# A mixer's hand-written order: low-rank gates a tile sooner, keys times decay as an event of its own, chunk products a part later, the states' last two reads a tile sooner with buffers of their own

## The reference

```python
h = modulate(rms_norm(x, g_norm1[l]), shift1, scale1)
proj = h @ w_in[l]
sb_q, sb_k, sb_v, gq, gk, gv, gg, gf = jnp.split(proj, offsets, axis=-1)
o_sb = stick_breaking_attention(...)                       # 8 heads of 64
log_alpha = jax.nn.log_sigmoid(gf @ w_fg2[l] + b_fg2[l]) / GLA_TAU
o_gla = gla_chunk_causal(gq, gk, gv, log_alpha)            # 4 heads, 8 chunks of 64 tokens
oh = oh * lax.rsqrt(jnp.mean(oh * oh, axis=-1, keepdims=True) + EPS)
o_gla = (oh * g_gla_out[l]) * jax.nn.silu(gg)
mixed = jnp.concatenate([o_sb, o_gla], axis=-1) @ w_out[l]

# inside gla_chunk_causal
k_dec = kc * jnp.exp(total[:, :, None] - cum)              # keys times decay
chunk_kv = jnp.einsum('bnchk,bnchv->nbhkv', k_dec, vc)     # chunk products
state = decay[..., None] * state + kv
o = jnp.einsum('bnchk,nbhkv->bnchv', qc, states)           # the states' reads
```

## Time and profile before

| what | us |
| --- | --- |
| median of 3 runs | 1533.07 (1532.12 to 1535.98) |
| the profiled execution, its own time | 1533.55 |
| span of its instructions | 1531.8 |
| PE busy | 1480.5 (97%) |
| DVE, ACT busy | 785.8 (51%), 550.9 (36%) |
| granted TensorE clock, mean | 0.977 of 2.4 GHz |
| the mixer's events, first tile to the first matmul of the output projection | 852.9 to 1099.4 |

### The profile page before, as it was taken

How to read it: one execution, slowest core, us unless ns; L and a number is a source line. 1 busy time by engine, 2 the same in 40 slices (tenths; PEclk the granted TensorE clock), 3 DMA queues, 4 the chain that set the end, 5 groups by cost and what they waited for, 6 DMA issues and landing times.

```text
span 1531.8 us, 18223 instructions
## 1 busy us (share of the span) xinstructions
PE 1480.5 (97%) x6646; PEld 1199.9 (78%) x6646; DVE 785.8 (51%) x1013; ACT 550.9 (36%) x699; POOL 25.0 (2%) x48
## 2 busy tenths in 40 slices
PE   6999999999999999999999896999899999999998
PEld 5887888888888888888888774666677888888886
DVE  7345454466455454544555654454356653563564
ACT  4343212223234413323143423335334542552342
POOL 1000000000000000000000000000000000000000
PEclk8999999999999999999999998999899999999998
DMA  5323544334432344352422221111022232323221
GB/s 172 109 88 107 176 160 156 123 116 163 161 110 86 107 129 146 104 170 82 150 83 83 83 79 31 55 56 55 28 83 82 85 107 82 110 93 98 90 76 55
DMA packets 135789, 158.18 MB, mean 103 GB/s; under 512 B 2513, under 2 KB 129071, under 8 KB 135743
## 3 DMA queue, kind: packets, MB, share of 16 engines
q1 hardware_dynamic: 129024, 131.08, 26.4%
q0 software_dynamic: 6240, 26.30, 5.1%
q10 hardware_dynamic: 479, 0.17, 0.0%
HBM read 155.44 MB, written 2.10 MB: 103 GB/s over the span
## 4 chain that ended last, share of the span: by engine, by line
PE 93%; DVE 3%; ACT 2%; DMA 1%; issue 1%; SPq 0%; DVEq 0%; ACTq 0%
PE bank L436 29%; PE bank L438 28%; PE bank L437 28%; DMA raw<-in_w_in 1%; ACT weights_hi L784 1%; PE bank L716 1%; PE aux L471 1%; PE aux L716 1%; PE aux L740 1%; PE aux L458 1%; PE aux L505 1%; PE aux L651 0%; DVE weights_lo L1113 0%; PE aux L546 0%; PE bank L726 0%
## 5 line engine op out<-in xcount | busy, mean ns | idle before, releaser
L436 PE MATMUL bank<-operand_hi,weights_hi 128*128 128x512 f32 x1936 | 767.3, 396 | 8.1 <-DVE operand_lo L1125 5.5
L438 PE MATMUL bank<-operand_hi,weights_lo 128*128 128x512 f32 x1936 | 758.2, 392 | 0.0
L437 PE MATMUL bank<-operand_lo,weights_hi 128*128 128x512 f32 x1936 | 758.0, 392 | 0.0
L436 PEld LDWEIGHTS bank<-operand_hi,weights_hi 128*128 128x128 f32 x1936 | 366.6, 189 | 93.2 <-issue 16.8
L438 PEld LDWEIGHTS bank<-operand_hi,weights_lo 128*128 128x128 f32 x1936 | 366.1, 189 | 77.6
L437 PEld LDWEIGHTS bank<-operand_lo,weights_hi 128*128 128x128 f32 x1936 | 366.9, 189 | 75.2 <-issue 1.0
L1113 DVE TENSOR_TENSOR weights_lo<-raw,weights_hi 128x1024 fp32r<-128x1024 f32 (+1 forms) x244 | 296.1, 1214 | 172.9 <-ACT weights_hi L784 167.3
L784 ACT ACTIVATE weights_hi<-raw 128x1024 fp32r<-128x1024 f32 (+1 forms) x244 | 253.6, 1045 | 300.5 <-PE bank L438 300.1
L789 ACT ACTIVATE operand_hi<-value 128x512 f32 (+1 forms) x90 | 56.9, 633 | 128.8 <-DVE value L1301 34.0
L1123 DVE TENSOR_TENSOR operand_lo<-value,operand_hi 128x512 fp32r<-128x512 f32 (+1 forms) x90 | 62.0, 689 | 42.5 <-ACT operand_hi L789 42.5
L1543 DVE SCALAR_TENSOR_TENSOR conv_or_gate<-bank,vector_table,conv_or_gate 128x511 f32<-128x511 f32 x44 | 32.9, 747 | 80.9 <-ACT conv_or_gate L1070 79.0
(11 more groups left out here) (206 smaller groups left out, 697.6 us busy)
## 6 DMA issues: line engine op xcount, KB each, us to landing
raw<-in_w_in SPq DMA_DIRECT2D x40, 1024.0 KB, 5.2
raw<-in_w_ff SPq DMA_DIRECT2D x32, 1024.0 KB, 5.2
ada_or_attention<-in_w_ada POOLq DMA_DIRECT2D x16, 1536.0 KB, 7.7
raw<-in_w_up SPq DMA_DIRECT2D x22, 1024.0 KB, 5.1
raw<-in_w_out SPq DMA_DIRECT2D x8, 1024.0 KB, 5.0
raw<-in_w_down SPq DMA_DIRECT2D x8, 1024.0 KB, 5.0
raw<-in_w_proj_a SPq DMA_DIRECT2D x4, 1024.0 KB, 6.4
raw<-in_w_proj_b SPq DMA_DIRECT2D x4, 1024.0 KB, 6.5
```

What stands on the lines that cost most here:

```text
L436: pe.matmul(dst[:, :], wh, ah, start=(kt == 0), stop=False)
L437: pe.matmul(dst[:, :], wh, al, start=False, stop=False)
L438: mm = pe.matmul(dst[:, :], wl, ah, start=False, stop=(kt == k_tiles - 1))
```

## The change

Five things, all in the mixer:

- `fg 0`, `fg 1`, `fg 2` stand ahead of tiles 5, 6 and 7 where they stood behind them. The two memsets that the scan needs go from tile 5's share of DVE to tile 4's.
- Keys times decay is an event of its own, `k_dec n`, one part ahead of `turn_k n`. For PE and ACT it is empty.
- `kv 0` to `kv 3` come one part later (`kv 0` and `kv 2` at the first part of tiles 15 and 16, `kv 1` and `kv 3` at the third).
- `o 2` and `o 3` go from the second and third part of tile 22 to the first and second part of tile 21, `ms 2` and `ms 3` from tile 23 to (21, 2) and (22, 0), `gated 0` and `gated 1` from (22, 0) to (22, 1).
- `o 2` and `o 3` get buffers of their own, `gk[0]` and `gk[1]` in the space of `mix_bias`, in place of `tA[0]` and `tA[1]`; and since ACT's squares go through `tb(n % 2)`, ACT now waits for L1477 of `ms n - 2` ahead of the square of `o n`.

The number and shapes of the instructions stay. The core of the diff:

```diff
-    others = {(9, 3): [("turn_k", 0)], (10, 3): [("turn_k", 1)],
+    others = {(9, 2): [("k_dec", 0)], (9, 3): [("turn_k", 0)], (10, 2): [("k_dec", 1)], (10, 3): [("turn_k", 1)],
...
-    order += [("tile", 4), ("turn_v", 3), ("tile", 5), ("fg", 0), ("tile", 6), ("fg", 1), ("tile", 7), ("fg", 2)]
+    order += [("tile", 4), ("turn_v", 3), ("fg", 0), ("tile", 5), ("fg", 1), ("tile", 6), ("fg", 2), ("tile", 7)]
...
+        scaled = [tA[0][:, :], tA[1][:, :], gk[0], gk[1]]
...
                 elif kind == "o":
                     act.wait_ge(aux2_filled, AUX2[event] + 1)
+                    if n >= 2:
+                        act.wait_ge(g_scaled, n - 1)
                     act.activation(tb(n % 2), aux[2][:, :], ACT.Square).then_inc(o_sq, 1)
...
-                    if n == 5:
+                    if n == 4:
 
                         dve.memset(spread[:, :], 1.0).then_inc(reset_ready, 1)
...
-                elif kind == "turn_k":
+                elif kind == "k_dec":
                     dve.wait_ge(g_dec, 2 * n + 2)
                     dve.wait_ge(*mix_slot(("gk", n)))
                     dve.tensor_tensor(gate_y[n], gk[n], gate_y[n], ALU.mult).then_inc(k_dec, 1)
+                elif kind == "turn_k":
                     keep_turned(event, k_tok.rearrange("p (b n) -> p b n", b=NBLK)[:, :, n * P:(n + 1) * P])
...
-                    dve.tensor_scalar(tA[n % 2][:, :], aux[2][:, :], col(C_GGLA + n), None, ALU.mult).then_inc(aux2_read, 1)
+                    dve.tensor_scalar(scaled[n], aux[2][:, :], col(C_GGLA + n), None, ALU.mult).then_inc(aux2_read, 1)
```

More of the change, by code:

```diff
@@ L91, in mixer_schedule @@
               (19, 3): 9, (20, 3): 10, (21, 3): 11, (22, 3): 12, (23, 3): 13}
-    others = {(9, 3): [("turn_k", 0)], (10, 3): [("turn_k", 1)],
+    others = {(9, 2): [("k_dec", 0)], (9, 3): [("turn_k", 0)], (10, 2): [("k_dec", 1)], (10, 3): [("turn_k", 1)],
               (11, 1): [("turn_gv", 0)], (12, 1): [("turn_gv", 1)], (13, 1): [("turn_gv", 2)], (14, 1): [("turn_gv", 3)],
[1 row of a table removed]
[1 row of a table added]
               (19, 1): [("o", 0)], (20, 0): [("o", 1)], (20, 1): [("ms", 0)], (20, 2): [("ms", 1)],
[2 rows of a table removed]
[1 row of a table added]
+              (22, 1): [("gated", 0), ("gated", 1)]}
     order = [("tile", 0)]
@@ L1040, in _ @@
                     act.wait_ge(value, VALUED["gla"] + n + 1)
-                    round_operand(0, 4 + n, tA[n % 2][:, :])
+                    round_operand(0, 4 + n, scaled[n])
                 elif kind == "z":
@@ L1473, in _ @@
                     dve.wait_ge(o_sq, n + 1)
-                    dve.tensor_scalar(tA[n % 2][:, :], aux[2][:, :], col(C_GGLA + n), None, ALU.mult).then_inc(aux2_read, 1)
+                    dve.tensor_scalar(scaled[n], aux[2][:, :], col(C_GGLA + n), None, ALU.mult).then_inc(aux2_read, 1)
                 elif kind == "ms":
                     dve.wait_ge(g_inv, n + 1)
-                    dve.tensor_tensor(tA[n % 2][:, :], tA[n % 2][:, :], tb(n % 2), ALU.mult).then_inc(g_scaled, 1)
+                    dve.tensor_tensor(scaled[n], scaled[n], tb(n % 2), ALU.mult).then_inc(g_scaled, 1)
                 elif kind == "gated":
@@ L1482, in _ @@
                         dve.wait_ge(tri_done, N_ITEMS)
-                    dve.tensor_tensor(tA[n % 2][:, :], tA[n % 2][:, :], yb[:, n * S:(n + 1) * S], ALU.mult).then_inc(value, 1)
-                    rest(0, 4 + n, tA[n % 2][:, :], MADE["gla"] + n)
+                    dve.tensor_tensor(scaled[n], scaled[n], yb[:, n * S:(n + 1) * S], ALU.mult).then_inc(value, 1)
+                    rest(0, 4 + n, scaled[n], MADE["gla"] + n)
                 elif kind == "z":
```

## The result

The changed kernel takes 1522.76 us (median of 4 runs, 1521.82 to 1523.59) against 1532.9 us before (4 runs). The ratio is 0.9936 with a 95% interval of 0.9923 to 0.9949: 10 us faster, 8 to 12. The forecast was 9.3 us.

The account below looks back on a forecast made before the run. PE works all but 3% of the span, so gains come only from its gaps and clock. Terms +7.1 - 8.7 - 1.2 - 6.5 = -9.3 gave 1523.8 us from the median 1533.07, range 1517.5 to 1530.

Parts of the forecast that it names:

- three signs of being wrong: No wait before the low-rank product, clock low for longer than 10 us, or a low clock from the `o 3` wait.
- The gates a tile sooner: New 5.4 us gap before the low-rank product: `tri 0` 4.8 us late plus 2.3 of low clock, +7.1.
- Keys times decay: At `turn_k`, waits of 3.5 and 3.6 us and 1.7 of clock go, 0.1 comes back: -8.7 us.
- Chunk products: PE reaches the chunk products a part later, which covers their 1.2 us wait: -1.2 us.
- The last two reads: At `o 3`, a 3.7 us wait and 4.5 of clock go, a new 1.7 us wait comes: -6.5 us.
- Gaps of 1.2 left no low clock: New 1.7 us wait before `o 3` was given no clock cost, with 4.5 us as the other bound.
- The third rival: ACT's chain behind Silu takes 2.8 us more, so `tri 11` waits 1.5: 1525.3 us; chance 0.02.
- The gates come sooner after all: Copy of last v does not hold PE; gate chain starts 5.4 us sooner, +7.1 becomes -0.8: 1516 us; chance 0.05.
- Gains are given back to the clock: Gaps of 5.4, 4.3 and 1.7 us each leave low clock costing 4.5: 1532 us, no change; chance 0.09.
- Slower: Low clock after the low-rank gap does not end, up to `z 1`: about +29 for 2.3, 1550 us; chance 0.04.

Follow-up runs that it names:

- e1: Kernel before with only the gates a tile sooner and their memsets at tile 4: 1537.86 us, ratio 1.0044.
- e5: Changed kernel with DVE's copy of the last turned v ahead of tile 4's share: 1514.83 us, ratio 0.9891 to the kernel before.
- e2: Kernel before with only keys times decay as its own event, one part ahead of `turn_k`: 1523.6 us, ratio 0.9947.
- e6: Kernel before with only the chunk products a part later: 1532.45 us in one run.
- e3: Kernel before with only the last two reads a tile sooner, with their own buffers: 1527.53 us, ratio 0.9966.
- e10: Changed kernel run a third time, unedited: 1525.43 us in one run, against 1530.68 for the kernel before on that chip.
- e7: Changed kernel with gates 0 and 1 in old order and the second gate behind item 1 and `turn_k 0`: 1509.7 us, ratio 0.9851 to before.
- e4: Changed kernel with the gates back in their old order, all else kept: 1515.62 us, ratio 0.9896 to the kernel before.
- e12: Kernel before with only the last two reads sooner, run again unedited: 1525.54 us once, against 1530.24 for the kernel before on that chip.
- e11: Changed kernel with gates in old order, run again unedited: 1517.46 us once, against 1530.24 for the kernel before on that chip.

## Why the prediction was right, point by point

**The whole.** Forecast 1523.8, measured 1522.76. Part of the agreement is luck. In the two profiled executions the mixer gained 8.1 us (212.1 to 204.0), 1.2 less than forecast; the spans differ by 11.8, and the other 3.7 lie outside the mixer, 0.9 ahead of `turn_v 3` and 2.8 behind `pv 11`, where the change moves nothing. The 0.9 is idle time of PE. Behind `pv 11` PE has 3.8 us less busy time at the same matmuls (422.2 to 418.4), with a granted clock of 0.97 before and 0.99 after, and 1.0 more idle time.

Of the three signs of being wrong that the prediction names, two stayed away: the wait before the low-rank product is there, and no low clock in the mixer lasted longer than 10 us (the longest, behind the gap before `o 3`, took 6.8). The third came: the wait before `o 3` did cost a low clock. The time was right all the same, since the miss was small.

**The gates a tile sooner, +7.1 forecast.** The gap was 5.0 where 5.4 was reckoned. The small memset ran beside the copy, and the copy started 1.99 us after the scalings where it was 1.31 before, so 0.7 later and not 0.8; and the transposes end 0.6 us after their start, by their row, where the prediction took 0.4. The clock behind it cost 1.4, not 2.3. `tri 0` came 44.7 us after `turn_v 3` where it was 38.9, 5.7 later (4.8 + 2.3 was forecast), and its wait fell to 4.1, where the prediction had 4.3 (its own terms, 5.1 + 4.8 - 5.4, give 4.5). The clock behind `tri 0`, left at 3.1, was 2.3. The sign, the place and the releaser were right, and e1 alone (6.7 us slower) and e5 (the gap closed by the place of one copy) show the cause.

**Keys times decay, -8.7 forecast.** e2 alone gave 8.1 by the ratio and 10.7 in its mixer, which differs from the forecast also by 1.4 us of clock behind the gap before `o 3` and 0.8 behind `tri 0` that this profile did not have. Both waits went, 0.2 came back where 0.1 was forecast. In the changed kernel the way from `tri 0` to `pv 8` is 10.6 us shorter (132.97 to 122.41); without the 1.2 of the chunk products and the 0.8 of clock behind `tri 0`, 8.6 are left for this part.

**Chunk products, -1.2.** Gone in the changed kernel and in e6.

**The last two reads, -6.5 forecast.** From `pv 8` to `pv 11` it was 40.2 us (1057.82 to 1098.01) and is 37.0: 3.2 gained. This is the term that was mis-sized, in the step "Gaps of 1.2 left no low clock, and this one is nearer to it than to 3.5; I add nothing for it, 4.5 as the other bound". The wait was 1.6 as forecast (1.7), but a low clock followed that cost 3.4 us, within the bound. Over nine profiles it costs 1.3 on the mean, which alone makes the term 5.2. The 4.5 that was to go away was mis-sized too: it is the largest of four profiles with the old gap, whose mean is 3.7. With both means the term is about 4.5. e3 measured 5.2 (3.4 to 7.2), which tells none of these figures from another. `tri 11` did not wait, by 1.4 us where 1.3 was reckoned. The third rival, a longer chain behind Silu, is out: from PE's start of `z 11` to the end of item 11 it took 9.3 us (1068.77 to 1078.05), as in the rows of before, and behind each of the two table loads of 1.28 us the next activation began 1.29 us after the load's start, as before.

**The rivals.** "The gates come sooner after all" fell with the 5.0 us wait, and e5 shows what it would have taken: one copy moved, and then 1514.83, where the rival gives 1516. "Gains are given back to the clock" came true at one of its three gaps, with 3.4 us for its 4.5; at the other two the clock cost 1.4 and 2.3. "Slower" did not: the low clock behind the low-rank gap cost 1.4 us, so it ended within three us of matmuls with 16 columns of weights, and the longest of four profiles was 5.4 us (e10). That rival's price does not come out of its own terms either: 11.1 and as much again, less 4.3, is 17.9 and not 29, and 23 us of low clock would take PE through the product and one tile (22.2 us) and not through three and a half. No run bears on that price.

**What I did not see.** The forecast priced the gates at +7.1 and so said that the change was better without them. Nor did it ask whether `tri 0`'s wait could be had at all, which e7 did: by taking the second gate out from ahead of item 0 and not by moving both.

## What to carry to other kernels

When an in-order engine waits through one shared buffer, moving a step ahead gains nothing if the read that frees the buffer stays where it is in the other engine's queue: look up which instructions stand ahead of that read, and move the read (5.0 us to 0.8 by one copy). Even that only took back the loss here: e5 is no faster than the old order of the gates (e4). The gain lay in what item 0 itself stood behind (e7, 5.1 us to 0.9). A product that one engine needs soon should stand ahead of the housekeeping that needs the latest tile (7.1 us of waits for two reordered instructions). And price the parts of a change one by one: this one was 10 us faster as a whole, with one part that cost 6.

## What the runs showed of the hardware

The four waits of PE in the changed kernel's mixer repeat to 0.1 us over three profiles (5.0, 4.1, 1.6, 0.2); the one at the norm ahead of it does not (2.5, 2.5, 3.0). Nor does the clock: after gaps of 4.1 us and more it was low in all 16 places seen, at a cost of 1.3 to 3.1 us; after 3.5 to 3.7 us in 12 of 14, with 1.4 to 4.6; after 1.6 us, ahead of a read made of 64x64 matmuls, in 5 of 9, with 1.7 or 3.4; after 1.2 us in none of 5. The same kernel showed it and did not show it at the same gap (e3 and e12, e4 and e11). What in an execution decides it stays open.
